# Projecting the values first and bringing the input in a token tile at a time in a hybrid attention layer

## The reference, cut to what matters

```
h    = rmsnorm(x) * norm_g
proj = h @ w_in                 # w_in is 1024 x 6912
a_qkv, z_a, b_qkv, z_b, r_a, r_b = split(proj)
3 groups x 4 heads: dilated sliding-window attention, merged by their softmax denominators
8 heads: block-sparse causal attention
y_a = (attn_a * silu(z_a)) @ w_pa ;  y_b = (attn_b * silu(z_b)) @ w_pb
merged = sigmoid(r_a + b_merge[:D]) * y_a + sigmoid(r_b + b_merge[D:]) * y_b
out    = rmsnorm(x + merged @ w_out) * final_g
```

## Time and profile before

| | us |
|---|---|
| median of 3 runs | 461.39 |
| the profiled execution | 461.4 |
| its span (first to last instruction) | 459.6 |
| TensorE busy in the span | 443.7 (97%) |
| VectorE, ScalarE, GpSimd busy | 218.0, 193.8, 166.7 |

### The profile page before, as it was taken

One profiled execution on the slowest core, in us unless ns is written; L12 is line 12 of the kernel. 1 busy time (PEld: TensorE's weight loads), 2 busy tenths in 40 slices (PEclk: granted clock), 3 DMA queues, 4 the chain that ended last, 5 costly groups with the idle time before them and its releaser, 6 DMA issues.

```text
span 459.6 us, 6290 instructions
## 1 busy us (share of the span) xinstructions
PE 443.7 (97%) x2417; PEld 379.8 (83%) x2417; DVE 218.0 (47%) x347; ACT 193.8 (42%) x392; POOL 166.7 (36%) x106
## 2 busy tenths in 40 slices
PE   7899999999999999999799999899999999999995
PEld 7689998899889888987678888688888888888885
DVE  3981243313203355668977767905207074073433
ACT  5743553344325444666336555323323253242111
POOL 3545332324234243555326552435434346300000
PEclk9999999999999999999899999999999999999998
DMA  8822252024202232122022022213322272320331
GB/s 280 270 91 93 92 139 92 2 93 138 92 9 85 93 93 93 32 73 93 21 73 83 8 70 73 65 63 121 116 70 91 91 250 95 138 91 0 123 106 46
DMA packets 38444, 43.07 MB, mean 94 GB/s; under 512 B 3448, under 2 KB 35216, under 8 KB 38416
## 3 DMA queue, kind: packets, MB, share of 16 engines
q1 hardware_dynamic: 35968, 42.47, 28.3%
q10 hardware_dynamic: 2448, 0.21, 0.4%
HBM read 39.48 MB, written 2.15 MB: 91 GB/s over the span
## 4 chain that ended last, share of the span: by engine, by line
PE 91%; DVE 4%; ACT 2%; DMA 1%; issue 1%; SPq 0%; DVEq 0%; ACTq 0%
PE ps L708 19%; PE ps L709 19%; PE ps L712 19%; PE ps L752 4%; PE ps L753 4%; PE ps L754 4%; PE ps L913 3%; PE ps L912 3%; PE ps L911 3%; PE ps L828 3%; PE ps L808 3%; PE ps L855 3%; PE ps L845 2%; PE ps L811 2%; DMA xs<-in_x 1%; DVE gat_lo L1237 1%
## 5 line engine op out<-in xcount | busy, mean ns | idle before, releaser
L636 POOL TENSOR_TENSOR w_lo<-raw,w_hi 128x1024 fp32r<-128x1024 f32 (+1 forms) x59 | 138.9, 2355 | 195.3 <-ACT w_hi L928 188.7
L708 PE MATMUL ps<-hT_hi,w_hi 128*128 128x512 f32 x336 | 137.9, 411 | 6.3 <-ACT w_hi L928 2.7
L709 PE MATMUL ps<-hT_hi,w_lo 128*128 128x512 f32 x336 | 133.3, 397 | 0.0
L712 PE MATMUL ps<-hT_lo,w_hi 128*128 128x512 f32 x336 | 133.2, 396 | 0.0
L708 PEld LDWEIGHTS ps<-hT_hi,w_hi 128*128 128x128 f32 x336 | 63.6, 189 | 18.5 <-ACT w_hi L928 5.2
L712 PEld LDWEIGHTS ps<-hT_lo,w_hi 128*128 128x128 f32 x336 | 63.5, 189 | 15.3
L709 PEld LDWEIGHTS ps<-hT_hi,w_lo 128*128 128x128 f32 x336 | 63.8, 190 | 11.4
L928 ACT CAST w_hi<-raw 128x1024 fp32r<-128x1024 f32 (+1 forms) x59 | 60.1, 1019 | 19.4 <-PE ps L712 16.6
L752 PE MATMUL ps<-w_hi,hT_hi 128*128 128x256 f32 x160 | 46.0, 287 | 0.0
L754 PE MATMUL ps<-w_lo,hT_hi 128*128 128x256 f32 x160 | 44.7, 279 | 0.0
L753 PE MATMUL ps<-w_hi,hT_lo 128*128 128x256 f32 x160 | 44.7, 279 | 0.0
(11 more groups left out here) (141 smaller groups left out, 661.1 us busy)
## 6 DMA issues: line engine op xcount, KB each, us to landing
raw<-in_w_in SPq DMA_DIRECT2D x25, 1024.0 KB, 5.0
raw<-in_w_out SPq DMA_DIRECT2D x4, 1024.0 KB, 4.8
xs<-in_x SPq DMA_DIRECT2D x4, 512.0 KB, 5.3
raw<-in_w_pb SPq DMA_DIRECT2D x4, 512.0 KB, 4.1
res<-in_x SPq DMA_DIRECT2D x4, 512.0 KB, 4.1
out<-weighted SPq DMA_DIRECT2D x8, 256.0 KB, 2.1
raw<-in_w_in SPq DMA_DIRECT2D x2, 512.0 KB, 9.1
raw<-in_w_pa SPq DMA_DIRECT2D x4, 256.0 KB, 3.0
```

What stands on the lines that cost most here:

```text
L636: nc.gpsimd.tensor_tensor(ring(w_lo, n, kt), src, ring(w_hi, n, kt).bitcast(F32), ALU.subtract).then_inc(lo_ready, 1)
L708: pe.matmul(out, wh, hh, start=(k == 0), stop=False)
L709: pe.matmul(out, wl, hh, start=False, stop=False)
L712: return pe.matmul(out, wh, hl, start=False, stop=(k == kts - 1))
```

## The change

1. The first unit has the chunk order v, k, q like the others.
2. SyncE issues x tiles 0 and 1, weight chunk 0 in one piece, x tiles 2 and 3, weight chunk 1, and then the rest.
3. `norm_g` is loaded as one row on one partition. TensorE spreads it over all partitions by two fp32 products of a column of ones with it (1 row deep, 512 columns each) into PSUM banks 6 and 7, after 8 warming products instead of 14. `scale_rows` becomes a `scalar_tensor_tensor` that multiplies by the row's `rstd` and by the spread `norm_g` read from PSUM.
4. Each token tile is turned, and split over all its channels at once: one copy of 128x1024 on ScalarE (`input_highs`) and one subtraction of 128x1024 on VectorE (`input_lows`). The transposes alternate between PSUM banks 2-3 and 4-5.
5. Steps 0 and 1 run `first_values`: for each of two token tiles, eight high x high products, then eight low x high, then eight high x low, with waits of their own. The transposes of tile 2 stand behind the fourth of step 0's six parts and those of tile 3 behind the last.
6. GpSimd's cast of step 1's high part waits for the whole chunk and counts on a semaphore of its own, as does VectorE's low part of step 0. GpSimd's low part of step 1 no longer waits for VectorE's low part of step 0; it waits for ScalarE's high part of step 0 (`highs_before(2)` is 1).

The diff, cut to its core:

```diff
-    CHUNKS += [("k", q + w), ("q", q), ("v", q + 2 * w)] if u == 0 else [("v", q + 2 * w), ("k", q + w), ("q", q)]
+    CHUNKS += [("v", q + 2 * w), ("k", q + w), ("q", q)]
-WARM = 14
+WARM = 8
+def highs_before(n):
+    return n if n < 2 else n - 1
+def lows_before(n):
+    return max(n - 1, 0)
+        def x_banks(i):
+            return ps[:, XB + 2 * (i % 2):XB + 2 * (i % 2) + 2, :]
+        def x_blocks(i):
+            return x_banks(i).rearrange("p b (k c) -> p (b k) c", c=P)
 @block.sync
-            for i in range(TT):
-                sp.dma_start(xs[:, i, :], x_t[:, i, :]).then_inc(x_in[i], 16)
+                for i in ((0, 1) if n == 0 else (2, 3) if n == 1 else ()):
+                    sp.dma_start(xs[:, i, :], x_t[:, i, :]).then_inc(x_in[i], 16)
 @block.gpsimd
             def lows(n):
-                pool.wait_ge(hi_ready, n + 1)
+                pool.wait_ge(hi_ready, highs_before(n + 1))
...
-            pool.wait_ge(hi_ready, 1)
-            pool.wait_ge(first_half_in[1], 16)
+            pool.wait_ge(raw_in[0], 16)
             src, kt = raw_half(1)
-            nc.gpsimd.tensor_copy(ring(w_hi, 1, kt), src).then_inc(hi_ready, 1)
-            pool.wait_ge(lo_ready, 1)
+            nc.gpsimd.tensor_copy(ring(w_hi, 1, kt), src).then_inc(pool_hi_ready, 1)
+            pool.wait_ge(pool_hi_ready, 1)
 @block.tensor
+            pe.wait_ge(ones_ready, 1)
+            pe.wait_ge(g_in, 16)
+            for e in range(2):
+                last = pe.matmul(ps[:, GB + e, :], ones[:, :], g_row[:, 512 * e:512 * e + 512], start=True, stop=True)
+            last.then_inc(g_spread, 1)
+            pe.wait_ge(vec_in, 16)
+            pe.transpose(ps[:, 1, 0:16], vecs[:, :], ident[0:16, 0:16]).then_inc(vecs_turned, 1)
+            def turn_x(i):
                 pe.wait_ge(x_scaled, i + 1)
+                if i >= 2:
+                    pe.wait_ge(hT_lo_ready, i - 1)
                 for k in range(KT_D):
-                    last = pe.transpose(ps[:, k, P * i:P * i + P], xs[:, i, P * k:P * k + P], ident[:, :])
+                    last = pe.transpose(x_blocks(i)[:, k, :], xs[:, i, P * k:P * k + P], ident[:, :])
                 last.then_inc(x_turned, 1)
+            turn_x(0)
+            turn_x(1)
...
+                def first_values(i, part):
+                    t = 2 * n + i
+                    if part == 0:
+                        pe.wait_ge(hT_hi_ready, t + 1)
+                        pe.wait_ge(hi_ready, 1)
+                        pe.wait_ge(pool_hi_ready, 1)
+                        if n == 1:
+                            pe.wait_ge(hbias_ready, 1)
+                    elif part == 1:
+                        pe.wait_ge(hT_lo_ready, t + 1)
+                    else:
+                        pe.wait_ge(dve_lo_ready, 1)
+                        pe.wait_ge(lo_ready, 1)
+                    o = ps[:, pbank(n), UW * i:UW * i + UW].rearrange("p (j c) -> p j c", j=2)
+                    for k in range(KT_D):
+                        h = (hT_lo if part == 1 else hT_hi)[:, k, P * t:P * t + P]
+                        w = pair_ring(w_lo if part == 2 else w_hi, n)[:, :, P * k:P * k + P]
+                        last = pe.matmul(o, h, w, start=(part == 0 and k == 0), stop=(part == 2 and k == KT_D - 1))
...
+                if n < 2:
+                    pieces = [lambda i=i, part=part: first_values(i, part) for i in range(2) for part in range(3)]
+                    if n == 0:
+                        pieces[4:4] = [lambda: turn_x(2)]
+                        pieces += [lambda: turn_x(3)]
 @block.scalar
+            def input_highs(i):
+                act.wait_ge(x_turned, i + 1)
+                nc.scalar.copy(hT_hi[:, :, P * i:P * i + P], x_blocks(i)).then_inc(hT_hi_ready, 1)
+            for i in range(2):
+                square(i)
+                root(i)
+            input_highs(0)
+            highs(0)
+            input_highs(1)
+            for i in range(2, TT):
+                square(i)
+                root(i)
+            input_highs(2)
+            input_highs(3)
 @block.vector
+            def scale_rows(i):
+                dve.wait_ge(rstd_ready, i + 1)
+                if i == 0:
+                    dve.wait_ge(g_spread, 1)
+                nc.vector.scalar_tensor_tensor(out=xs[:, i, :], in0=xs[:, i, :], scalar=rstd[:, i:i + 1],
+                                               in1=ps[:, GB:GB + 2, :].rearrange("p b c -> p (b c)"),
+                                               op0=ALU.mult, op1=ALU.mult).then_inc(x_scaled, 1)
+            def input_lows(i):
+                dve.wait_ge(hT_hi_ready, i + 1)
+                cols = slice(P * i, P * i + P)
+                nc.vector.tensor_tensor(hT_lo[:, :, cols], x_blocks(i), hT_hi[:, :, cols].bitcast(F32),
+                                        ALU.subtract).then_inc(hT_lo_ready, 1)
+            for i in range(2):
+                variance(i)
+                scale_rows(i)
+            dve.wait_ge(vecs_turned, 1)
+            nc.vector.tensor_scalar(hbias[:], ps[:, 1, 0:16], 0.5, None, ALU.mult).then_inc(hbias_ready, 1)
+            input_lows(0)
             dve.wait_ge(hi_ready, 1)
             src, kt = raw_half(0)
             nc.vector.tensor_tensor(ring(w_lo, 0, kt), src, ring(w_hi, 0, kt).bitcast(F32),
-                                    ALU.subtract).then_inc(lo_ready, 1)
+                                    ALU.subtract).then_inc(dve_lo_ready, 1)
+            input_lows(1)
+            for i in range(2, TT):
+                variance(i)
+                scale_rows(i)
+            for i in range(2, TT):
+                input_lows(i)
```

More of the change, by code:

```diff
@@ L384, in hybrid_layer_program @@
         x_in = [sem(f"x_in{i}") for i in range(TT)]
+        g_in = sem("g_in")
         vec_in = sem("vec_in")
+        ones_ready = sem("ones_ready")
+        g_spread = sem("g_spread")
+        pool_hi_ready = sem("pool_hi_ready")
+        dve_lo_ready = sem("dve_lo_ready")
         fg_in = sem("fg_in")
         raw_in = [sem(f"raw_in{i}") for i in range(NRAW)]
-        first_half_in = [sem(f"first_half_in{i}") for i in range(2)]
         const_step = sem("const_step")
@@ L458, in hybrid_layer_program, with raw_waits @@
         out_t = out.rearrange("b (n p) d -> p (b n) d", p=P)
[L460 to L463 removed]
+        def raw_waits(item):
             n = LOAD_OF[item]
@@ L467, in raw_waits @@
                 k, c = LOADS[m]
-                count += 0 if m == 0 else 32 if k == "w" and CHUNKS[c][0] == "y" else 16
+                count += 32 if k == "w" and CHUNKS[c][0] == "y" else 16
             return raw_in[n % NRAW], count
@@ L718, in start @@
                 def start():
-                    weights_wait(n)
-                    if kind == "v":
+                    if n >= 2:
+                        weights_wait(n)
+                    if kind == "v" and n >= 2:
                         weights_wait(n // 2 * 2 + 1)
@@ L756, in value_rows @@
                         last.then_inc(projected, 1)
+                def first_values(i, part):
[16 more added lines that the diff above has]
+                        last = pe.matmul(o, h, w, start=(part == 0 and k == 0), stop=(part == 2 and k == KT_D - 1))
+                    if part == 2 and i == 1:
+                        last.then_inc(projected, 1)
                 def branches(ks):
@@ L920, in highs @@
             def highs(n):
-                s, count = raw_waits(("w", n // 2), n % 2)
+                s, count = raw_waits(("w", n // 2))
                 act.wait_ge(s, count)
-                if n == 2:
-                    act.wait_ge(hi_ready, 2)
                 if n >= NRING:
@@ L938, in wo_highs, with square @@
                 nc.scalar.copy(wo("hi", k), raw_out(k)).then_inc(wo_hi_ready, 1)
-            act.dma_start(vecs[0:8, :], norm_g.rearrange("l (k p) -> (l k) p", p=P)).then_inc(vec_in, 16)
-            act.dma_start(vecs[8:24, :], b_merge.rearrange("l (k p) -> (l k) p", p=P)).then_inc(vec_in, 16)
+            act.dma_start(g_row[:, :], norm_g[:, :]).then_inc(g_in, 16)
+            act.dma_start(vecs[:, :], b_merge.rearrange("l (k p) -> (l k) p", p=P)).then_inc(vec_in, 16)
             act.wait_ge(consts_ready, 1)
             nc.scalar.activation(unread[:], ident[:, 0:1], ACT.Sqrt)
-            for i in range(TT):
+            def square(i):
                 act.wait_ge(x_in[i], 16)
@@ L949, in _, with root @@
                                      accum_out=ss[:, i:i + 1]).then_inc(squared, 1)
+            def root(i):
                 act.wait_ge(var_ready, i + 1)
                 nc.scalar.activation(rstd[:, i:i + 1], rvar[:, i:i + 1], ACT.Sqrt).then_inc(rstd_ready, 1)
-            highs(0)
-            act.wait_ge(x_turned, TT)
-            act.wait_ge(gb_ready, 1)
-            for k in range(KT_D):
-                nc.scalar.activation(hT_hi[:, k, :], ps[:, k, :], ACT.Copy,
-                                     scale=gb[:, k:k + 1]).then_inc(hT_hi_ready, 1)
+            def input_highs(i):
```

(19 more changed lines are left out.)

52 lines of the change are left out of this document (16 added, 36 removed).

## The result

The kernel after takes 465.15 us (median of 20 executions, 463.20 to 466.84); 20 executions of the kernel before on the same chips take 462.20 us (460.72 to 464.46). The ratio is 1.0043, with a 95% interval of 1.0026 to 1.0060: slower by 2.0 us (1.2 to 2.8). The medians lie 2.95 us apart, because the executions of both kernels fall into groups and a median jumps from one group to the next; so the ratio is what counts here. The forecast of +1.5 us lies within the interval, and the ratio lies within the 0.5% given, though the interval reaches past it. The median of 465.15 us as such is 2.25 us above the forecast's 462.9 and just above 465.0, the top of its range; 0.8 us of this is the kernel before, whose median of three was that much lower than its median of twenty.

A forecast was written before the change was run, and what follows sets the result against it. TensorE, busy 97% of the span, was taken as the bound, with step 1's end deciding. First product at 12.3 (-2.8), turning +1.8 and stalls 1.5 and 1.0 gave +1.5 on 461.4: 462.9 us, range 460.2 to 465.0.

The forecast's parts named there:

- The sum: At step 1's end: first product 2.8 us earlier, turning +1.8, stalls 1.5 and 1.0, giving 27.85 - 26.31 = +1.5 us.
- The place and the mechanism: Weights' low parts in steps 0 and 1: VectorE's subtraction stands until GpSimd's finishes, ending at E + 4.49; chance 0.45.
- the rival without a meeting: The two low parts don't delay each other; step 1 ends at 25.9, -0.4 us, 461.0; chance 0.27.
- if that point stays: Spreading of `norm_g`: the clock still rises near 6.5 us, so spreading ends and tile 0's scaling starts at 7.65.
- Turning 1.13: Tile 0's transposes on TensorE, with hand-overs, take 1.13 us after its scaling at 8.87, ending at 10.06.
- E: End of ScalarE's copy of tile 0's high part from PSUM, forecast for 11.07 us.
- S: Start of TensorE's first product in step 0, forecast for 12.3 us, 2.8 us earlier than before.
- cold start: At the spreading the clock stays at 1.2 GHz past 6.6 us; step 1 ends at 29.6, +3.3 us, 464.7; chance 0.18.
- The order v, k, q: First unit's chunk order costs nothing in step 6; exponentials move about 0.5 us, within more than 2 us of slack.

The follow-up runs named there:

- e1: Kernel after, with GpSimd's low part of step 1 waiting until VectorE's low part of step 0 is done; median 464.54 us, ratio 1.0019 to before.
- e4: Kernel after, with VectorE making both low parts of weight chunk 0 and scaling tile 2 before tile 1's low part; 463.52 us, ratio 1.0011 to before.
- e3: Kernel after without the multiplication by `norm_g`, scaling by the old `tensor_scalar`, the spreading still run; 461.00 us, ratio 0.9998 to before.
- e9: Kernel after with e4's low parts, 4 warming products before the spreading and 4 filling ones behind it; 462.90 us, ratio 0.9998 to before.
- e10: Kernel after without `norm_g`'s multiplication or spreading, with 14 warming products and e4's low parts; 460.59 us, ratio 0.9955 to before.
- e5: Kernel after with spreading products 128 rows deep, the row's load having to wait for a zeroed tile; 466.26 us, ratio 1.0076 to before.
- e6: Kernel after with e5's 128-row spreading and late row load, plus e4's low parts; 465.71 us, ratio 1.0074 to before.
- e11: Kernel after with e4's low parts, spreading by four fp32r products of the split row, 7 warming and 3 filling products; 461.21 us, ratio 0.9962 to before.
- e2: Kernel after with six more identity products between the spreading and the first transposes; 466.27 us, ratio 1.0080 to before.
- e7: Kernel after with `norm_g` brought by a 512 KB broadcast load, no spreading, 14 warming products and e4's low parts; 462.52 us, ratio 0.9997 to before.
- e8: Kernel after with spreading products 128 rows deep, VectorE copying the row into a zeroed tile in time; 463.76 us, ratio 1.0029 to before.

## Why the prediction was right

The sum came out as +1.5 and the profile shows +2.0 at the start of step 2, with +1.8 in the execution's time. The path forecast is that of this execution and of the eight others of 463.2 to 463.6 us; the remaining eleven are slower by 1.5 to 3.6 us. That all twenty together still come out at +2.0 is in part luck: the kernel before has executions up to 464.46, for reasons that the forecast didn't have either. Step by step:

- **The place and the mechanism were right.** The first product was forecast for 12.3 (12.40), VectorE's low part for 3.4 us (3.39), part 2 for 15.75 (15.98), a wait of 1.5 ahead of it (1.45), tile 2 scaled at 18.55 with a wait of 1.0 (18.87 and 0.79), step 2 at 27.85 (28.31). e1 shows the mechanism by taking it away: 1.22 us alone. e4 shows its worth together with the queue behind it, 1.85 us; the rival without a meeting had 27.85 - 25.9 = 1.95.
- **The first product was right by luck, by errors that cancel.** The step "if that point stays": the level rose at 4.2 and not at 6.5 us, so tile 0 was scaled from 7.00 and not from 7.65. The step "Turning 1.13": TensorE stood 1.44 us behind the spreading, fell to 1.2 GHz, and from the end of the scaling (8.28) to E (11.36) it took 3.1 us and not 2.2. So E came 0.29 us late. A third error hides that: the sum ended the weights' high part at 12.0 and put S at 12.3, with 0.3 us that it did not work out; the high part ended at 12.30 and the first product followed 0.10 later.
- **The 0.46 us missing at step 2** begin at E, 11.36 and not 11.07 (+0.29); VectorE's low part ends at E + 4.56 and not E + 4.49 (+0.07). From the turning of tile 2 on, two turnings cost 0.85 and 0.80 us and not 0.90 (-0.15), and the eight parts of products 7.74 us and not 7.48 (+0.26): they are 0.95 apart and not 0.935, and the part behind a turning costs 1.02 to 1.03.
- **The cold start was rated too low.** It had a chance of 0.18 and +3.3 us. Of the five profiled executions with the spreading of the kernel after and its 8 warming products, three had it (e1, e3, e4). It costs tile 0's scaling 9.13 - 7.00 = 2.1 us, so step 2 of the kernel after would start at 30.4 with it, +4.1, where the rival had 29.6. The rival's E was 12.85 and is 13.48 in e1 and e4: a warming record costs 0.23 us at the low level and not 0.21, so the spreading begins at 5.24 and not 4.9, and it ends at 9.02 and not 8.55. The 20 executions of the kernel after fit: nine at 463.2 to 463.6, ten at 465.1 to 465.4, which is 2 us more, one at 466.8. No slow one of them was profiled, so that the cold start makes the upper groups is likely, not shown.
- **What the prediction did not see** is a second place where the level is decided, in the middle of the kernel. Behind the wait of 2.72 us in the kernel before the products stay 0.43 us apart until 228.4; the kernel after keeps the level behind the same wait (2.52 us) and loses it behind one of 1.84:

```profile
227.33 0.47 PE L732 MATMUL ps<-hT_hi,w_hi 128*128 128x512 f32 x1 [2.52 <-DVE KTs L1236]
...
293.92 0.47 PE L732 MATMUL ps<-hT_hi,w_hi 128*128 128x512 f32 x1 [1.84 <-DVE zf L1271]
...
295.19 0.63 PE L733 MATMUL ps<-hT_hi,w_lo 128*128 128x512 f32 x1
```

The granted clock shows both places: it is 0.50 for 3 to 4 us behind the wait near 225, or behind the one near 294, or behind both. From step 2 to the end of the span it is 432.9 to 433.3 us in the profiled executions with one such stretch (before, e9 and e10 near 225; after, e3, e5, e6 and e11 near 294), and 434.6 to 434.8 in those with two (e1, e2, e4, e7 and e8). So each loss costs about 1.5 us. The length of the wait alone does not say which, so a time of one execution is uncertain by 1.5 us for a reason far from the change. The order v, k, q costs nothing that can be seen in step 6, as forecast: the lag of the kernel after stays at 1.9 to 2.0 us (ScalarE's high parts of the same step start at 56.04 and 57.93, and at 124.86 and 126.84).

The Trainium skill, TensorE: Matmul & The Clock Gate, Part 4: PE-mode transpose, says that transposes don't count as activity. The runs speak against it for these fp32 turnings: in the kernel after and in e4 the level rises while TensorE does nothing but turn (421 ns from 8.3 to 10.8 us, then 273), and in e8 two turnings behind stands of 1.29 and 0.72 us keep it. Since the level can rise some time behind the work (e6), the kernel after is the stronger case: there the last other work ended 4.2 us before the rise. For the meeting of the low parts, the Trainium skill, SBUF — State Buffer, Who interferes with whom, says that a VectorE instruction with two SBUF inputs contends with a GpSimd one that reads SBUF and that the second to issue is blocked until the first has finished: 3.39 us against 1.22, and the 743 ns of the kernel before's subtractions from PSUM beside GpSimd's and behind it, agree with it.

## What to carry to other kernels

A wait between two engines that looks like mere order may keep two SBUF subtractions apart: one engine doing both (2.35 us) can be quicker than two side by side (3.39). Count what a new operand needs to get to its place: here the order by token tiles was worth 1.55 us at the end of step 1 as long as no operand had to be brought (e10), and the row's way there cost 1.7, about 0.9 of it the low level. Where work depends on TensorE's level, price it at both levels, since executions of one kernel differ in it.

## What the runs showed of the hardware

- TensorE worked without a pause from 1.52 to 8.9 us in e1, e3 and e4 and was at 1.2 GHz all the time, with spreading products one row deep from 5.2 on; with full-depth products alone it had risen by about 7 us in all three kernels.
- The moment of the rise differs between executions with the same work: 4.9 us in e10 and 6.5 in before and e7 behind the same start of the warming, 4.2 in the kernel after and not by 5.2 in e1. The level can rise while TensorE stands (e6, between 5.3 and 7.25).
- The level can be lost over a stand of 1.44 us (after) and kept over one of 2.52 us (after, 227.33) in the same execution.
- A VectorE subtraction of two SBUF tensors of 128x1024 took 1.22 us alone and 3.36 to 3.39 us (e2, e3, e8, after) when it began just behind a GpSimd subtraction of the same size; with one operand in PSUM (128x512) it took 743 ns either way.
- The broadcast load of 512 KB took 5.4 us to land; against e10 it moved x tile 1's scaling from 7.53 to 9.79 us and chunk 0's cast from 10.04 to 11.03.
